# A trunk layer of attention, two recurrences and a mixture of experts: most input column blocks and both recurrences run eleven slots later, and expert rows are summed in DRAM

## The reference

```
x   = layer_norm(x)
z   = x @ w_in                       # 1024 x 3252, split into the inputs of three mixers
ya  = attention over the top 256 keys of a scored selection (72 keys for the sample)
yb  = chunked gated linear attention (state carried)      # a recurrence
yc  = chunked mLSTM (state carried)                       # a recurrence
x   = layer_norm(ALPHA * x + concat(ya, yb, yc) @ w_out)
gate, e = router(x)                  # two of 16 experts for each token
out = 0
for e in range(16):
    out += gate[:, e] * (silu(x @ w_gate[e]) * (x @ w_up[e])) @ w_down[e]
y   = layer_norm(ALPHA * x + out)
```

## Time and profile before

| what | us |
|---|---|
| median of 3 runs (1431.27 to 1437.92) | 1431.75 |
| the profiled execution | 1436.13 |
| its span, first to last instruction | 1434.5 |
| TensorE busy | 1222.2 (85%) |
| VectorE busy | 763.7 (53%) |
| ScalarE, GpSimd busy | 394.0, 431.3 |
| mean granted TensorE clock, share of full speed | 0.882 |

### The profile page before, as it was taken

How to read it: one execution, slowest core, us unless ns; L and a number is a source line. 1 busy time by engine, 2 the same in 40 slices (tenths; PEclk the granted TensorE clock), 3 DMA queues, 4 the chain that set the end, 5 groups by cost and what they waited for, 6 DMA issues and landing times. The chain is left out here.

```text
span 1434.5 us, 16391 instructions
## 1 busy us (share of the span) xinstructions
PE 1222.2 (85%) x5725; PEld 789.7 (55%) x5725; DVE 763.7 (53%) x1787; ACT 394.0 (27%) x805; POOL 431.3 (30%) x460
## 2 busy tenths in 40 slices
PE   5899899999999999999989899889662999999500
PEld 2466566655755755755665464366322878778300
DVE  0024223777878878897889788942511000000088
ACT  1142432424224225222331431142110221211111
POOL 5112124134044045046005401210212221121787
PEclk9999999999999989898989898955675999999855
DMA  9965854544635525344343333400001999998163
GB/s 280 320 209 190 290 160 158 161 147 160 184 96 195 156 90 167 116 146 135 115 127 102 117 102 115 146 2 15 15 20 50 350 346 315 329 315 313 41 236 124
DMA packets 147610, 238.62 MB, mean 166 GB/s; under 512 B 17019, under 2 KB 119330, under 8 KB 147538
## 3 DMA queue, kind: packets, MB, share of 16 engines
q1 hardware_dynamic: 131298, 197.66, 43.4%
q0 software_dynamic: 10064, 29.16, 6.6%
q10 hardware_dynamic: 6176, 10.88, 2.1%
HBM read 211.38 MB, written 26.29 MB: 166 GB/s over the span
## 5 line engine op out<-in xcount | busy, mean ns | idle before, releaser
L1191 PE MATMUL bank_pair<-win,xT 128*128 128x384 f32 (+7 forms) x1152 | 445.3, 537 | 12.8 <-DMA win<-in_w_in 11.7
L1191 PEld LDWEIGHTS bank_pair<-win,xT 128*128 128x128 f32 (+1 forms) x1152 | 210.4, 191 | 187.0 <-issue 95.1
L900 DVE MAX8 top<-score 128x8 f32<-128x384 f32 (+6 forms) x201 | 174.9, 870 | 4.0
L901 DVE MATCH_REPLACE8 score<-top,score 128x384 f32<-128x384 f32 (+6 forms) x201 | 172.0, 856 | 0.0
L1285 PE MATMUL bank_pair<-w_out,yT 128*128 128x512 f32 (+1 forms) x288 | 131.8, 612 | 0.4 <-ACT yT L626 0.4
L570 POOL TENSOR_TENSOR small<-small,pexp 128x4 f32<-128x4 f32 (+1 forms) x9 | 9.4, 1049 | 331.0 <-DVE small L1081 331.0
L1285 PEld LDWEIGHTS bank_pair<-w_out,yT 128*128 128x128 f32 (+1 forms) x288 | 52.9, 187 | 74.5 <-issue 72.9
L1642 DVE TENSOR_TENSOR hT<-gate,bank_pair 128x160 f32<-128x160 f32 x32 | 10.3, 321 | 149.3 <-ACT gate L1586 149.3
L1145 PE MATMUL bank_pair<-ident,lm 128*128 128x128 f32 (+2 forms) x234 | 43.2, 312 | 45.9 <-ACT lm L736 15.9
L1554 POOL DMA_INDIRECT xg<-x_rows,ids x32 | 30.0, 937 | 160.7 <-PE bank_pair L1660 142.3
L1145 PEld LDWEIGHTS bank_pair<-ident,lm 128*128 128x128 f32 (+2 forms) x234 | 31.7, 171 | 58.7 <-issue 32.6
(11 more groups left out here) (341 smaller groups left out, 2022.8 us busy)
## 6 DMA issues: line engine op xcount, KB each, us to landing
win<-in_w_in SPq DMA_DIRECT2D x90, 768.0 KB, 4.4
win<-in_w_in SPq DMA_DIRECT2D x18, 1024.0 KB, 5.4
win<-in_w_in SPq DMA_DIRECT2D x18, 840.0 KB, 5.0
win<-in_w_in SPq DMA_DIRECT2D x18, 800.0 KB, 4.6
wg<-in_w_exp_gate SPq DMA_DIRECT2D x12, 1024.0 KB, 12.7
wu<-in_w_exp_up SPq DMA_DIRECT2D x12, 1024.0 KB, 16.5
wd<-in_w_exp_down SPq DMA_DIRECT2D x12, 1024.0 KB, 16.8
expert_rows<-rows ACTq DMA_DIRECT2D x16, 512.0 KB
```

Of the source, the lines that this page charges most:

```text
L900: step(V.max(top8[0:n], sc))
L901: step(V.match_replace(sc, top8[0:n], sc, NEG))
L1191: last = mmul(zb[0:n, 0:w], xT[:, kk, 0:n], win[:, i % NWIN, k, 0:w], start=(kk == 0), stop=(kk == KD - 1))
```

## The change

- `tile_strands` goes; a new `weave` starts every strand of every tile at its own global slot (`STARTS`). `project` is split: `project_a` keeps the transposes, the two attention blocks (halves in slots 1 to 4), turns and scores; `project_b` has the six other blocks and starts 11 slots (`SHIFT`) later, with halves in its slots 0 to 7 and 12 to 15. `recur(t)` starts 11 slots later than before, so it ends in slot 10 of the stretch of `attend(t)`. `attend`, `route` and `select` keep their stretches.
- `xT` gets two buffers, `x0` has one instead of two, and is loaded one tile ahead.
- Logits are made in slots 0, 1, 3, 5 (`LOGIT_SLOT`) and go by turns to `lm` and to `yT` (`probs`), so that a head's reduction waits for the turns of the head before the last. `ROUNDS` is dealt out anew. Placing moves to slot 4 of `route` and waits for `fm_ready` of the next tile's recurrence; the recurrence's slot 12 waits for `slots_ready` of the tile before.
- For the sample tile each input block and the output matmul are cut into four column quarters, written to four groups of 32 partitions; ScalarE's copies and the residual addition take them one by one.
- Rows of x1 are also written to `sum_rows` in DRAM: by a DRAM to DRAM copy in `route`, for the sample straight from the core. `slot_tokens` holds pairs of token number and gate; empty slots name one of 128 spare rows.
- Experts: loops are unrolled. Slots of all experts are loaded at the start (`id_h`, `id_a`, `id_b`); weights of experts 1 to 3 come after that. Expert rows are multiplied by gate / ALPHA while they are copied and are added to `sum_rows` by indirect DMAs with an add. GpSimd's multiplication by ALPHA goes. When all is added, SP loads the sums as `xr`.
- `combine` becomes `finish_rows`: ScalarE takes the sum and the sum of squares, GpSimd makes the power, VectorE makes two passes, SP stores.

The diff, cut to its core:

```diff
+SHIFT = 11
+ATT_CUTS = 2
+HALF_SLOT_A = [1, 2, 3, 4]
+HALF_SLOT_B = [0, 1, 2, 3, 4, 5, 6, 7, 12, 13, 14, 15]
+STARTS = {"attend": lambda t: SLOTS_T * (t + 2), "route": lambda t: SLOTS_T * (t + 3), "recur": lambda t: SLOTS_T * (t + 1) + SHIFT,
+          "project_b": lambda t: SLOTS_T * t + SHIFT, "project_a": lambda t: SLOTS_T * t, "select": lambda t: SLOTS_T * (t + 1)}
...
-PLACE_SLOT = 3
+PLACE_SLOT = 4
...
-ROUNDS = [0, 1, 1, 2, 2, 3, 2, 3, 2, 3, 2, 2, 4, 2, 2, 1, 0, 0]
+ROUNDS = [0, 1, 1, 2, 2, 1, 2, 3, 3, 3, 2, 3, 1, 1, 2, 3, 2, 0]
+LOGIT_SLOT = [0, 1, 3, 5]
...
+        probs = [lm[:], yT.rearrange("p k n -> p (k n)")]
...
+                        if t < NPT:
+                            pool.wait_ge(S("x1_stored"), 16 * t + 16)
+                            pool.dma_start(acc_d[128 * t:128 * t + n], x1_d[128 * t:128 * t + n]).then_inc(S("sum_begun"), 16)
...
-                        if h:
-                            dve.wait_ge(S("pT_ps"), groups_before(t) + ng * h)
+                        if h >= 2:
+
+                            dve.wait_ge(S("pT_ps"), groups_before(t) + ng * (h - 1))
...
+                    for q in range(QS):
+                        last = mmul(zb[SMP * q:SMP * q + SMP, 0:qs[q + 1] - qs[q]], xT[:, t % 2, kk, 0:n],
+                                    win[:, i % NWIN, k, qs[q]:qs[q + 1]], start=(kk == 0), stop=(kk == KD - 1))
...
-                        if t + 2 < NT:
-                            pe.wait_ge(S("vT_ready"), t + 3)
+
+                        if t + 1 < NT:
+                            pe.wait_ge(S("fm_ready"), t + 2)
...
                         done("fm_ready")
+                        if t:
+                            pe.wait_ge(S("slots_ready"), t)
...
+                def add_rows(e):
+
+                    if e:
+                        pool.wait_ge(S("added_a"), 16 * e)
+                        pool.wait_ge(S("added_b"), 16 * e)
+                    pool.wait_ge(S("oa_copied"), e + 1)
+                    pool.indirect_dma_start(
+                        out=acc_d, out_offset=bass.IndirectOffsetOnAxis(ap=id_a[:, e, 0:1], axis=0),
+                        in_=rows_a[e % 2][:], in_offset=None, compute_op=ALU.add).then_inc(S("added_a"), 16)
+                    pool.wait_ge(S("ob_copied"), e + 1)
+                    pool.indirect_dma_start(
+                        out=acc_q, out_offset=bass.IndirectOffsetOnAxis(ap=at_b[:, e:e + 1], axis=0),
+                        in_=rows_b[e % 2][:], in_offset=None, compute_op=ALU.add).then_inc(S("added_b"), 16)
...
+                for e in range(NE):
+                    if e + 2 < NE:
+                        pool.wait_ge(S("xgT_ps"), 4 * (e + 1))
+                        gather(e + 2)
+                    if e == 0:
+                        pool.wait_ge(S("slots_split"), 1)
+                    else:
+                        add_rows(e - 1)
+                add_rows(NE - 1)
...
+                    if e >= 2:
+                        act.wait_ge(S("added_a"), 16 * (e - 1))
+                    A.activation(rows_a[e % 2][:], OA[:], ACT.Copy, scale=w_a[:, e:e + 1]).then_inc(S("oa_copied"), 1)
...
+                A.activation(squares[0:tokens(t), t % 2, :], xr[0:tokens(t), t, :], ACT.Copy, accum_out=TOTAL(t)).then_inc(S("total_ready"), 1)
...
+                A.activation(squares[0:n, t % 2, :], xr[0:n, t, :], ACT.Square, bias=NMU(t), accum_out=SS(t)).then_inc(S("ss_ready"), 1)
...
+                    V.scalar_tensor_tensor(out=y2[0:n, t, :], in0=xr[0:n, t, :], scalar=NMU(t), in1=g2[0:n], op0=ALU.add,
+                                           op1=ALU.mult).then_inc(S("y_gained"), 1)
...
+                    V.scalar_tensor_tensor(out=y2[0:n, t - 1, :], in0=y2[0:n, t - 1, :], scalar=RSTD(t - 1), in1=b2[0:n], op0=ALU.mult,
+                                           op1=ALU.add).then_inc(S("y_ready"), 1)
```

More of the change, by code:

```diff
@@ L49 @@
 NW = 4
+SPARE = 128
 NEG = -1.0e30
@@ L134, in build @@
         win = keep("win", [128, NWIN, KD // 2, WCUT])
[L135 to L136 removed]
+        trunk(nc, a, o, win, ident, ones, chosen_sum, expert, before, token_gate, ps, x1_d, acc_d, slot_d)
+        experts(nc, a, o, win, ident, ones, chosen_sum, expert, before, token_gate, ps, x1_d, acc_d, slot_d, em_d)
 SLOTS_T = 18
 ORDER = [0, 1, 7, 4, 5, 2, 3, 6]
[L152 to L156 removed]
+SHIFT = 11
@@ L187, in use, with trunk @@
+USES, CUT_AT = bank_order()
+LAST_CUT = max(CUT_AT, key=lambda c: CUT_AT[c])
 def use(t, what, which):
-    return 2 + sum(len(bank_uses(u)) for u in range(t)) + bank_uses(t).index((what, which))
-def trunk(nc, a, o, win, ident, ones, chosen_sum, expert, before, gatew, ps, x1_d, slot_d):
+    return USES[t, what, which]
+def trunk(nc, a, o, win, ident, ones, chosen_sum, expert, before, token_gate, ps, x1_d, acc_d, slot_d):
     ctx = ExitStack()
@@ new lines, in project_b @@
+            def project_b(t):
+                n = tokens(t)
+                cout = o["conv_p"] if t < NPT else o["conv_s"]
+                for s in range(SLOTS_T):
+                    if s in HALF_SLOT_B:
+                        half = HALF_SLOT_B.index(s)
+                        load_half(t, ATT_CUTS + half // 2, half % 2)
+                    if s == 10 and t >= NPT - 1:
+                        sp.wait_ge(S("p_copied"), use(t, "cut", ORDER.index(5)) + 1)
+                        sp.dma_start(cout[0, 0], zc[n - 3:n, :]).then_inc(S("conv_stored"), 16)
+                    yield
@@ new lines, in _ @@
+                with nc.allow_non_contiguous_dma("slots"):
+                    for b in range(2):
+                        pool.dma_start(id_h[b][:, 0:1], slots_e[HALF * b:HALF * b + HALF, 0:1]).then_inc(S("halves0_loaded"), 16)
+                for q in range(QB):
+                    ins = nc.gpsimd.memset(quarter[CB * q:CB * q + CB], float(q))
+                ins.then_inc(S("quarter_set"), 1)
+                pool.wait_ge(S("halves0_loaded"), 32)
+                gather(0)
+                pool.wait_ge(S("halves_loaded"), 32)
```

644 lines of the change are left out of this document (341 added, 303 removed).

## The result

The changed kernel takes **1477.1 us** (median, 1474.3 to 1478.1), beside it the kernel before 1431.5: a ratio of 1.031, 95% interval 1.027 to 1.034. It is slower, where 1330 was forecast, and outside the forecast's range of 1292 to 1387. The profiled execution has a span of 1476.4 us, 41.9 more than that of before.

What follows compares the result with a forecast made beforehand. TensorE was taken to bound trunk (to 923 us, VectorE a close second) and experts. Trunk -63, experts +2 and end -41 sum to -102: 1334 us for the profiled execution, 1330 as median; range 1292 to 1387, own range 1305 to 1357.

Steps and rivals of the forecast that it cites:

- P0: Trunk, from tile 0's input transposes to tile 1's: loses five half blocks of TensorE work, -14 us.
- P1: Trunk, from tile 1's input transposes to tile 2's: loses 11 of 18 slots of the first recurrence, -14 us.
- P2 to P7: Trunk, tiles 2 to 7: fewer waits for the exponential and choice of experts, two waits added; -15 us (+10 to -30).
- P8: Trunk, tile 8's stretch: TensorE falls to about 91 us, VectorE keeps 104.5; 119 to about 107, -12 us (0 to -20).
- P9: Trunk, next to last stretch: more TensorE work between heads, shorter pause, clock above 0.8; -17 us (+3 to -27).
- P10: Trunk's last stretch: sample's recurrence beside its attention +18 us, quartered output matmul -9; together +9.
- experts: The 16 experts: 15.0 us each stays, small loads ahead of weights, adding DMAs hidden; +2 us (-4 to +8).
- end: After the last matmul: 88.3 us becomes 47.1, bound by ScalarE at 2.8 a tile; -41 us (-33 to -45).
- rival 1: Experts: the adding DMAs' chain sets the period, deciding from 13.5 us on; slower than before, up to 1502 us; chance 0.07.
- Rival 2: Experts: the DMA engines' load becomes the bound, a period of 17 us; +32, 1362 us; chance 0.12.
- Rival 3: Trunk: VectorE and the clock keep it, only P0 and P1 won; -20 for -63, 1373 us; chance 0.14.
- Rivals 4 and 5: Quartered records don't run side by side: +23, 1353 us, chance 0.04; TensorE keeps upper clock through P9: trunk -105, 1288, 0.05.

Runs made afterwards that it cites:

- e9: Changed kernel with block 5 (zc) instead of block 7 (zo) copied in slot 12, ahead of the recurrence's functions on ScalarE; 1421.0 us, ratio 0.987.
- e13: e9 plus a later deal of the selection rounds (11, 8, 6, 5, 2), halves where the change put them; 1384.7 us, ratio 0.959.
- e11: Kernel before with the changed experts and end and the quartered sample tile, its own order, rounds and single score buffer; 1382.1 us, ratio 0.958.
- e16: e15 with the weights of the first moved halves issued earlier on SP; 1379.8 us, ratio 0.958.
- e4: Changed kernel without the quartering of the sample tile's input blocks and output matmul; 1488.4 us, ratio 1.035.
- e15: e13 plus one block's two halves moved to slots 9 and 10; 1383.8 us, ratio 0.961.
- e6: Changed kernel with one block's two halves moved from slots 17 and 0 to slots 9 and 10; 1480.5 us, ratio 1.030.
- e14: e9 plus one block's two halves at slots 9 and 10, the changed kernel's own deal of rounds; 1420.8 us, ratio 0.984.
- e1: Changed kernel with its 32 selection rounds dealt later, 10 ahead of slot 9 for 15; 1462.0 us, ratio 1.015.

## Why the prediction was wrong

| step | forecast | measured |
|---|---|---|
| P0 | -14 | -2.0 (55.5 to 53.5) |
| P1 | -14 | -11.7 (73.4 to 61.7) |
| P2 to P7 | -15 | **+80.8** |
| P8 | -12 | **+21.2** |
| P9 | -17 | -11.3 |
| P10 | +9 | +7.3 |
| experts | +2 | -0.2 |
| end | -41 | -41.8 |
| sum | -102 | +41.9 (with -0.4 between the stretches) |

**The failed step is "P2 to P7".** It looked at the waits that the change removes (some 11 us) and at two semaphore waits that it adds, and bounded the term at +10. Neither added wait stands in the list of TensorE's waits. What it never asked is who the new neighbours in a slot are. The prediction said "Every tile's work stays within the same 12 stretches; when it runs is what moves", and took moving as free inside a full stretch. The runs put two pauses in its place: `zo`'s copy behind the recurrence on ScalarE, 41 us of the 81 (e9), and VectorE's rounds ahead of `ya` and `qk`, 38 more (e13). Together they return P2 to P7 to the length of before. Of the 81 us, 30 were not waiting but slow work (12.1 of 19.8 in P3), a cost that the prediction named in this very term for the waits that go ("after such a pause the clock stands low for a while") and left out for new ones.

**P8.** "VectorE keeps its 104.5, so P8 goes from 119 to about 107" was wrong twice. VectorE had 113.5 us, as part of the shifted recurrence came into the stretch. And it is never full: 109.0 of 123.2 us in e11, where only TensorE's work shrank, 107.9 of 127.9 in e13 without the pause of slot 12. So when TensorE's work shrinks here, VectorE's busy time is not the length that is left; its own waits, 14 us in e11, come on top. Four pauses of 7.1, 8.1, 13.4 and 14.2 us stand in P8, 42.8 of TensorE's 46.8 idle us.

**P0.** TensorE's busy time fell by 7 us only, at a mean clock of 0.87, and a pause of 11.0 us for weights came, which the prediction left out: the moved halves' loads are moved as well, past the small vectors in SP's queue. e16 puts about half of the pause down to that queue; the rest stays open.

**P1, P9, P10** came out within 6 us of their terms. The clock in P9 is 0.75, short of the 0.8 asked for. P10 holds its hops, and the quartered output matmul is 5.5 us, as in the 4.3 to 8.6 given; e4 puts the saving at 9.8 us for a forecast of 9. A quartered half measures 1.2 us (11.7 us for ten) for 1.5.

**Experts and end** came out within 2.2 and 0.8 us. The DMA issues of the changed kernel (us from issue to landing):

```profile
xg<-x_rows,id_h POOLq DMA_INDIRECT x32, 7.2
sum_rows<-rows_a,id_a POOLq DMA_INDIRECT x16, 10.3
sum_rows<-rows_b,at_b POOLq DMA_INDIRECT x16, 9.9
```

The adds land in 10.3 us for an estimate of 10, below the 13.5 from which rival 1 decides, so rival 1 fell. The experts' last matmuls are 14.9 us apart (1205.09 to 1428.86 for 15 steps) at a DMA share of 0.99, and TensorE waits 0.4 us for their weights in all. Rival 2 fell too, but nothing is to spare: where SP had 2.7 us between two sets, it now issues them back to back.

```profile
1291.09 3.46 SPq L1650 DMA_DIRECT2D win<-in_w_exp_down  x1
1294.60 0.98 SPq L1650 DMA_DIRECT2D wg<-in_w_exp_gate  x1
```

By the rule of the Trainium skill ("Collectives: The Full Stack", "The bandwidth ceiling: the fold count and why AG ≠ RS ≠ AR"), the adds would have taken about twice the plain store's time. Such a store landed in 6.6 us before and lands in 3.4 in the changed kernel's trunk; 10.3 is 1.6 to 3 times that, and no run here isolates the add. The prediction had the end's length right and its engine wrong: it is GpSimd's chain of two small rows a tile, 2.9 us, not ScalarE (2.4 us a tile). That is luck: the prediction priced ScalarE at 2.8 us a tile and GpSimd's power at 1.5 once. From the chain that ended last:

```profile
1464.07 1.30 POOL st L1976
...
1465.43 1.47 POOL st L1978
...
1466.99 1.30 POOL st L1976
```

**The rivals.** Rival 3 ("VectorE and the clock keep the trunk") named one of the two engines and the clock, but only as a gain that does not come, and nothing of ScalarE. No rival let the trunk become slower than before; the only slower one was in the experts, which is why the whole loss lay outside the range. e13 and e15 give rival 3's trunk: P2 to P7 unchanged, P0 and P1 won, P10 giving some back. Rivals 4 and 5 fell with a quartered half of 1.2 us and a clock of 0.75 in P9.

## What to carry to other kernels

When work is shifted in a slot schedule, write down for each engine what now stands in the same slot, in order, and price every hand-off whose slack shrinks: 5 slots between the recurrence's functions and the `zo` copy became none, and that one engine's order cost 56 us. Look at TensorE's busy time beside its idle time: a new pause can cost more than itself (81 us for 51 of idle time here), but idle time that is filled is not time won. Where halves were moved into a pause (e6, e14, e15), 14 to 17 us of idle time went and 9 to 19 us of busy time came. And rounds or other filler of a second engine have to be dealt anew against all of the meetings at once: e1 eased one and made another, and the largest gains in the trunk came from taking out the `zo` pause (56 us) and then dealing the rounds (36 us).
